# Sixteen unread products on TensorE in the routing stage of a two-block transformer kernel

## The chip, the cores and the metric

One core of a Trainium2 chip runs the whole kernel. The metric is the device time of one execution in microseconds, as the median of several runs. The granted clock of TensorE, which the profile gives as a share of full speed, has two levels: 0.50 (1.2 GHz) and 1.00 (2.4 GHz).

## The reference

Two blocks are computed one after the other on a sequence of 512 tokens of width 1024, in float32. The first is gated linear attention beside a convolution branch, the second is an mLSTM beside differential attention. The second block ends in an expert-choice feed-forward layer, and this is the part that matters here:

```
def expert_choice_ffn(h, w_router, w_gate, w_up, w_down):
    B, S, _ = h.shape
    cap = EC_CAPACITY * S // N_EXPERTS            # 2 * 512 / 16 = 64 tokens for each expert
    aff = jax.nn.softmax(jnp.einsum('bsd,de->bse', h, w_router).astype(jnp.float32), axis=-1)
    g, idx = lax.top_k(aff.transpose(0, 2, 1), cap)
    xe = h[bidx, idx]
    hid = (jax.nn.silu(jnp.einsum('becd,edf->becf', xe, w_gate))
           * jnp.einsum('becd,edf->becf', xe, w_up))
    ye = jnp.einsum('becf,efd->becd', hid, w_down) * g[..., None].astype(h.dtype)
    return jnp.zeros_like(h).at[bidx, idx].add(ye)
```

There are 16 experts, each with three weight matrices of 1024 x 2048 float32, so 24 MB of weights for each expert, 384 MB in all. The result is normalised and written out.

## The kernel before, in words

Every engine has one instruction stream of its own, written out by hand, and the streams wait for each other by counting semaphores (`t_dve`, `t_act`, `t_pe` in the routing, `x_...` and `e_...` in the experts). TensorE's stream has three stages.

**Dense blocks.** Up to about 1050 us TensorE multiplies the tiles of both blocks, mostly products of split operands (`d_hi`, `d_lo`) at line 2127.

**Routing**, from line 2405 to line 2434, about 1050 to 1068 us. `by_token` (line 2401) makes the router's logits in PSUM bank 3. `tokens_first` (line 2396) transposes the residual `xT` for one quarter of the tokens by eight transposes with the identity `ident`; three quarters go ahead of the ranking, the fourth, `tokens_first(3, 0)`, after it has been fed. ScalarE copies each quarter to `x2`, the tokens by row. VectorE computes the softmax `aff`; TensorE transposes it (line 2418, "affT"), and VectorE then ranks it: eight rounds of MAX8 (line 1931), with seven of MATCH_REPLACE8 (line 1933) between them, and three small steps that end in the limit `thr` for each expert (line 1936). TensorE waits for that at line 2422, transposes `thr` into bank 3 ("thrT", line 2423), VectorE marks the chosen tokens (lines 1939 and 1940), TensorE counts them by five products with a triangle and with ones (lines 2427 to 2432, "count"), and VectorE makes the positions `pos` and with them the selections `picks` (line 1954).

**Experts**, from line 2554. `gather(0)` (line 2442) multiplies `picks` by `x2`: eight products with 64 output partitions and 512 columns. ScalarE copies the result (`xg_first`), TensorE transposes it (line 2450), VectorE scales it to `xe` (line 1962), and then come the products with the weights, `gate_up` (line 2483) and `down` (line 2494), 64 and 32 of them for each expert, four for each 1 MB slot of weights. Each of them consists of two matmul records in the trace, and so does every product whose operands are plain float32; a transpose is one record.

The weights come on SyncE's queue alone, in the order of use, into a ring: `ring_a` and `ring_b` hold 22 slots of 1 MB, two more lie in `acc` and one in `once` (`ONCE = 3`, the fourth slot that is used). Filling starts long before the routing. The slots in `acc` wait for the last of the transposed tokens ("x3"), the one in `once` waits for "thrT". Every later transfer waits until TensorE has used the slot that it overwrites (`s_used`), the first of them until the first slot of expert 0 is used:

```
                    if g == ONCE:
                        sp.wait_ge(t_pe.sem, t_pe.count("thrT"))
                    elif order_of(g) >= RING + EXTRA:
                        sp.wait_ge(s_used, freed(g + n - 1))
```

All these waits of SyncE are in one order in one stream, the transfers too.

Of the kernel before, what the change touches and what calls it, by code (L numbers as in the profile page):

```python
# [14 lines left out]
S = 512  # L15
# [265 lines left out]
def kernel_program(nc, xT_in, pT_in, table, tri_in, gla_mask_in, rstm_in, negm_in, selr_in, m01_in, dist_in, tiles_in,  # L281
                   wgk_in, gkw_in, mgw_in, selg_in, diff_lam_2, w_router_2, experts_in, norm_f_g_2, x3_store, out):
    ctx = ExitStack()
    with ctx:
# [3 lines left out]
        def at(name, shape, kb, dt=F32):  # L288
            n = 4
            for d in shape[1:]:  # L290
                n *= d
            kb += 16 if kb >= 192 else 0
            assert base + kb * KB + n <= nc.sbuf_usable_end, (name, kb, n)
            return nc.alloc_sbuf_tensor_at(name, shape, dt, offset=base + int(kb * KB))
# [121 lines left out]
        x2 = at("x2", [P, TT, D], 64)  # L416
# [40 lines left out]
        ident = at("ident", [P, P], 192)  # L457
# [9 lines left out]
        ps = ctx.enter_context(nc.psum_tensor("ps", [P, 8, S], F32))  # L467
# [1555 lines left out]
        def _(pe):  # L2023
# [372 lines left out]
            def tokens_first(t, b):  # L2396
                for k in range(KD):
                    mm = pe.transpose(ps[:, b + k // 4, k % 4 * P:(k % 4 + 1) * P], xT[:, k, t * P:(t + 1) * P], ident[:, :])
                t_pe.done(mm, f"x{t}")

            def by_token(w, part, first):
                for t in range(TT):
                    tok = slice(t * P, (t + 1) * P)
                    mm = pe.matmul(ps[:, 3, t * 32:(t + 1) * 32], part[:, tok], w, start=first and t == 0, stop=True,
                                   skip_group_check=True)
                return mm

            pe.wait_ge(t_dve.sem, t_dve.count("part"))
            by_token(selm[:, :], lpart, True)
            read_done(pe, "out2", KD - 1)  # L2410
# [8 lines left out]
            t_pe.done(mm, "affT")  # L2419
            pe.wait_ge(t_act.sem, t_act.count("x0"))  # L2420
            tokens_first(3, 0)
            pe.wait_ge(t_dve.sem, t_dve.count("thr"))
            t_pe.done(pe.transpose(ps[:, 3, 0:NE], thr[:, 0:1].to_broadcast([NE, P]), ident[0:NE, 0:NE]), "thrT")
            pe.wait_ge(t_act.sem, t_act.count("ones"))
# [3 lines left out]
            for t in range(TT - 1):  # L2428
                pe.matmul(both[:, :, t + 1:, :], ones_r[:, :], chosen[:, :, t, :].unsqueeze(2).to_broadcast([P, 2, TT - 1 - t, NE]),
                          start=False, stop=False, skip_group_check=True)  # L2430
            pe.wait_ge(t_dve.sem, t_dve.count("gsum"))
            t_pe.done(pe.matmul(both[:, 1, :, :], ones[:, :], gsum[:, :].unsqueeze(1).to_broadcast([P, TT, NE]),
                                start=False, stop=True, skip_group_check=True), "count")
            pe.wait_ge(t_act.sem, t_act.count(f"x{TT - 1}"))

            def gather(e):
                if e >= 2:
                    pe.wait_ge(e_dve.sem, e_dve.count("o1", e - 2))
                for t in range(TT):
                    pe.wait_ge(x_dve.sem, x_dve.count(f"picks{t}", e))  # L2440
                    for d in range(2):
                        mm = pe.matmul(ps[d * CAP:(d + 1) * CAP, 5, :], picks[:, t, :], x2[:, t, d * S:(d + 1) * S],  # L2442
                                       start=t == 0, stop=t == TT - 1, skip_group_check=True)
                x_pe.done(mm, "gather")
# [281 lines left out]
```

## Time and profile before

| | |
|---|---|
| time, median of 3 runs | 1978.18 us (1977.48 to 1978.26) |
| the profiled execution: time | 1977.37 us |
| the profiled execution: span, first to last instruction | 1975.5 us |
| mean granted clock of TensorE | 0.99 |
| busy in the span | TensorE 96%, VectorE 37%, ScalarE 26%, GpSimd 3% |
| the chain that ended last | TensorE 73%, DMA 23%, ScalarE 2%, VectorE 1% |

The first lines say how long an execution takes; the time is 1.9 us more than the span in the profiled one. A busy share of TensorE says that its pipeline held a matmul, not that it ran at its peak. The chain is the sequence of work, followed back from the last instruction, in which each step released the next. In the rows below, an interval is given in microseconds from the span's start, PE is TensorE's matmuls, PEld its weight loads, DVE VectorE, ACT ScalarE, and SPq the transfers that SyncE issues. A name pair such as `ps<-x,picks` says which tensors an instruction writes and reads, and the shape behind it gives partitions and columns. What stands in square brackets at a row's end is how long the engine had been idle, and what released it.

### The profile page before, as it was taken

To read this page: it belongs to the slowest core of one execution; us is meant where nothing else is said; L and a number is where in the kernel's file an instruction comes from. 1 tells how busy PE (TensorE), PEld (TensorE's weight loads), DVE (VectorE), ACT (ScalarE), POOL (GpSimd) and SP (SyncE) were. 2 spreads that over 40 slices of the span, in tenths; PEclk is the share of its full clock that TensorE was granted. 3 is DMA by queue.
4 is the path that set the end of the run, shared out by engine and by line. 5 is a ranking of instruction groups with operands and counts; after the bars stand their busy time and mean duration, and the time that the engine had idled before them with its cause. 6 is when DMAs were issued, how large, how long until landed. Compare 5 with 4: busy or idle time off the path is not lost.

```text
span 1975.5 us, 20685 instructions
## 1 busy us (share of the span) xinstructions
PE 1888.2 (96%) x8735; PEld 1146.0 (58%) x8735; DVE 730.3 (37%) x1217; ACT 517.6 (26%) x837; POOL 61.2 (3%) x58
## 2 busy tenths in 40 slices
PE   8999999999999999999997999999888998989898
PEld 6788888888887888877874333333323333333332
DVE  7544444333356765777453111111111110111112
ACT  5444323222245353377622000000000000000002
POOL 1000000000014001100010000000000000000000
PEclk9999999999999999999998999999999999999999
DMA  5222322233322233121387999999999999999997
GB/s 189 86 86 64 118 96 96 96 98 98 109 94 100 82 109 127 55 71 46 138 329 306 421 433 431 432 432 433 434 432 432 432 432 434 432 432 432 431 429 295
DMA packets 49324, 504.93 MB, mean 256 GB/s; under 512 B 6416, under 2 KB 7440, under 8 KB 30544
## 3 DMA queue, kind: packets, MB, share of 16 engines
q1 hardware_dynamic: 48368, 502.49, 62.4%
q8 instruction: 69, 1.13, 0.2%
q10 hardware_dynamic: 864, 1.12, 0.2%
q14 instruction: 23, 0.19, 0.0%
HBM read 499.39 MB, written 4.19 MB: 255 GB/s over the span
## 4 chain that ended last, share of the span: by engine, by line
PE 73%; DMA 23%; ACT 2%; DVE 1%; issue 1%; ACTq 0%; SPq 0%; DVEq 0%
PE ps L2127 41%; DMA ring_a<-in_experts_in 23%; PE ps L2483 10%; PE ps L2494 6%; PE ps L2062 4%; PE ps L2442 3%; PE ps L2466 1%; PE ps L2304 1%; PE ps L2529 1%; PE ps L2280 1%; ACT hidT L1246 0%; PE ps L2505 0%; PE ps L2247 0%; PE ps L2230 0%; PE ps L2180 0%
## 5 line engine op out<-in xcount | busy, mean ns | idle before, releaser
L2483 PE MATMUL ps<-ring_a,xe 128*64 128x512 f32 x1504 | 343.0, 609 | 42.0 <-DMA ring_a<-in_experts_in 41.4
L2483 PEld LDWEIGHTS ps<-ring_a,xe 128*64 128x64 f32 x1504 | 107.0, 140 | 271.7 <-issue 211.9
L1291 DVE TENSOR_TENSOR d_lo<-d_raw,d_hi 128x1024 fp32r<-128x1024 f32 x166 | 206.1, 1250 | 120.4 <-ACT d_hi L851 119.5
L2127 PE MATMUL ps<-n_hi,d_hi 128*128 128x512 f32 x448 | 176.1, 393 | 1.5 <-DVE d_lo L1291 0.8
L2127 PE MATMUL ps<-n_lo,d_hi 128*128 128x512 f32 x448 | 174.4, 389 | 0.0
L2127 PE MATMUL ps<-n_hi,d_lo 128*128 128x512 f32 x448 | 174.3, 389 | 0.0
L851 ACT ACTIVATE d_hi<-d_raw 128x1024 fp32r<-128x1024 f32 x166 | 170.8, 1049 | 8.6 <-DMA d_raw<-in_tiles_in 6.4
L1521 DVE TENSOR_TENSOR hid<-hid,ps 128x512 f32<-128x512 f32 x32 | 20.7, 684 | 410.1 <-PE ps L2483 383.7
L1970 DVE TENSOR_TENSOR acc<-acc,ps 128x1024 f32<-128x1024 f32 x56 | 64.6, 1216 | 244.7 <-PE ps L2466 244.7
L2494 PE MATMUL ps<-ring_a,hidT 128*64 128x512 f32 x648 | 145.8, 596 | 9.3 <-DMA ring_a<-in_experts_in 6.2
L2483 PE MATMUL ps<-ring_b,xe 128*64 128x512 f32 x464 | 103.1, 594 | 3.0 <-DMA ring_b<-in_experts_in 2.9
L2494 PEld LDWEIGHTS ps<-ring_a,hidT 128*64 128x64 f32 x648 | 50.0, 137 | 90.3 <-issue 73.3
L2127 PEld LDWEIGHTS ps<-n_hi,d_hi 128*128 128x128 f32 x448 | 84.1, 188 | 19.7 <-DVE d_lo L1291 1.2
L2127 PEld LDWEIGHTS ps<-n_lo,d_hi 128*128 128x128 f32 x448 | 84.1, 188 | 17.5
L2127 PEld LDWEIGHTS ps<-n_hi,d_lo 128*128 128x128 f32 x448 | 84.1, 188 | 17.2
L2127 PE MATMUL ps<-h_hi,d_hi 128*128 128x512 f32 x224 | 89.4, 399 | 0.2 <-DVE d_lo L1291 0.2
L2127 PE MATMUL ps<-h_hi,d_lo 128*128 128x512 f32 x224 | 87.4, 390 | 0.0
L2127 PE MATMUL ps<-h_lo,d_hi 128*128 128x512 f32 x224 | 87.4, 390 | 0.0
L1237 ACT ACTIVATE xg<-ps 128x256 f32<-128x256 f32 x30 | 9.9, 382 | 292.9 <-PE ps L2442 292.9
L1243 ACT ACTIVATE hid<-ps 128x512 f32<-128x512 f32 x30 | 16.3, 594 | 258.7 <-PE ps L2483 258.7
L2483 PEld LDWEIGHTS ps<-ring_b,xe 128*64 128x64 f32 x464 | 33.0, 137 | 70.7 <-issue 65.8
L2494 PE MATMUL ps<-ring_b,hidT 128*64 128x512 f32 x304 | 68.2, 595 | 2.8 <-ACT hidT L1246 2.8
(505 smaller groups left out, 2719.9 us busy)
## 6 DMA issues: line engine op xcount, KB each, us to landing
ring_a<-in_experts_in SPq DMA_DIRECT2D x56, 4096.0 KB, 42.2
ring_b<-in_experts_in SPq DMA_DIRECT2D x28, 3072.0 KB, 42.5
d_raw<-in_tiles_in SPq DMA_DIRECT2D x166, 512.0 KB, 3.3
ring_a<-in_experts_in SPq DMA_DIRECT2D x31, 1024.0 KB, 12.9
ring_a<-in_experts_in SPq DMA_DIRECT2D x12, 2048.0 KB, 13.6
ring_b<-in_experts_in SPq DMA_DIRECT2D x5, 2048.0 KB, 13.5
ring_b<-in_experts_in SPq DMA_DIRECT2D x8, 1024.0 KB, 16.5
x_in<-in_xT_in SPq DMA_DIRECT2D x4, 512.0 KB, 7.2
```

What stands on the lines that cost most here:

```text
L851: act.activation(d_hi[:, n % SLOTS, :, :], d_raw[:, n % SLOTS, :, :], ACT.Copy).then_inc(t_hi, 1)
L1291: dve.tensor_tensor(d_lo[:, n % SLOTS, :, :], d_raw[:, n % SLOTS, :, :], d_hi[:, n % SLOTS, :, :].bitcast(F32), ALU.subtract).then_inc(t_l ...
L1521: return dve.tensor_tensor(out, a, b, ALU.mult)
L1970: e_dve.done(dve.tensor_tensor(row, old, ps[:, b:b + 2, :], ALU.add), f"o{t}")
L2062: mm = pe.matmul(bank, lt[:, k, t * P:(t + 1) * P], rhs, start=k == 0 and m == 0, stop=k == KD - 1 and m == 2)
L2127: mm = pe.matmul(bank, lt[:, n, gr.k0 + k, :], rt[:, k, :], start=k == 0 and m == 0, stop=k == gr.nk - 1 and m == 2)
L2280: mm = pe.matmul(ps[:, 5 + h % 2, q * P:(q + 1) * P], aaT[:, n % 2, c, :], d_tok[:, c, h * DDV:(h + 1) * DDV], start=c == 0, stop=c == TT - 1)
L2304: mm = pe.matmul(ps[:, 2 + i, :], dqT[half, h, q * P:(q + 1) * P], dkT[half, h, :], start=True, stop=True)
L2442: mm = pe.matmul(ps[d * CAP:(d + 1) * CAP, 5, :], picks[:, t, :], x2[:, t, d * S:(d + 1) * S], start=t == 0, stop=t == TT - 1, skip_group_ ...
L2466: return pe.matmul(ps[:, bank, :], place[half, t * P:(t + 1) * P], ye[half, :], start=start, stop=True, skip_group_check=True)
L2483: mm = pe.matmul(ps[half * CAP:(half + 1) * CAP, 2 * m + q, :], xe[:, k, :], slot(e, n)[:, (2 * q + half) * S:(2 * q + half + 1) * S], sta ...
L2494: mm = pe.matmul(ps[d * CAP:(d + 1) * CAP, 4, :], hidT[:, q, c, half * CAP:(half + 1) * CAP], slot(e, n)[:, j * D + d * S:j * D + (d + 1) ...
```

## The change

A helper `kept_busy(n)` issues n products of the identity (stationary) and the first 512 columns of the first quarter of `x2` (moving), all into PSUM bank 3, whose contents nobody reads. Fourteen stand between the last transposes of the tokens and the wait for `thr`, two between the counting products and `gather(0)`. Nothing else changes; no semaphore is signalled or awaited by them.

```
             def by_token(w, part, first):
...
+            def kept_busy(n):
+
+                for _ in range(n):
+                    pe.matmul(ps[:, 3, :], ident[:, :], x2[:, 0, 0:S], start=True, stop=True)
+
             pe.wait_ge(t_dve.sem, t_dve.count("part"))
...
             pe.wait_ge(t_act.sem, t_act.count("x0"))
             tokens_first(3, 0)
+            kept_busy(14)
             pe.wait_ge(t_dve.sem, t_dve.count("thr"))
             t_pe.done(pe.transpose(ps[:, 3, 0:NE], thr[:, 0:1].to_broadcast([NE, P]), ident[0:NE, 0:NE]), "thrT")
...
             t_pe.done(pe.matmul(both[:, 1, :, :], ones[:, :], gsum[:, :].unsqueeze(1).to_broadcast([P, TT, NE]),
                                 start=False, stop=True, skip_group_check=True), "count")
             pe.wait_ge(t_act.sem, t_act.count(f"x{TT - 1}"))
+            kept_busy(2)
 
             def gather(e):
```

TensorE's order in the routing before, from the last transposes of the tokens to the first products with weights (`thr` is the limit, `chosen` the marks, `gsum` their sums; x8 stands for eight in a row):

```order
L2398 MATMUL ps<-ident,xT 128x128 x8
L2423 MATMUL ps<-ident,thr 128x16
L2427 MATMUL ps<-chosen,tri_r 128x128
L2429 MATMUL ps<-chosen,ones_r 128x2x48
L2429 MATMUL ps<-chosen,ones_r 128x2x32
L2429 MATMUL ps<-chosen,ones_r 128x2x16
L2432 MATMUL ps<-gsum,ones 128x64
L2442 MATMUL ps<-x_161,picks 64x512 x8
L2450 MATMUL ps<-ident,xg_first 128x128 x4
L2483 MATMUL ps<-ring_a,xe 64x512 x12
```

The same place of the same engine after the change:

```order
L2398 MATMUL ps<-ident,xT 128x128 x8
L2411 MATMUL ps<-x_161,ident 128x512 x14
L2429 MATMUL ps<-ident,thr 128x16
L2433 MATMUL ps<-chosen,tri_r 128x128
L2435 MATMUL ps<-chosen,ones_r 128x2x48
L2435 MATMUL ps<-chosen,ones_r 128x2x32
L2435 MATMUL ps<-chosen,ones_r 128x2x16
L2438 MATMUL ps<-gsum,ones 128x64
L2411 MATMUL ps<-x_161,ident 128x512 x2
L2449 MATMUL ps<-x_161,picks 64x512 x8
L2457 MATMUL ps<-ident,xg_first 128x128 x4
L2490 MATMUL ps<-ring_a,xe 64x512 x12
```

The new rows are the two at line 2411. The order of everything else on TensorE, and that of ScalarE, VectorE and SyncE, is as before; line numbers behind the helper grow by five to seven.

## Rows read from the trace of the kernel before

**Rows 1.** The page: granted clock and GB/s in 40 slices of the span
```profile
PEclk9999999999999999999998999999999999999999
GB/s 189 86 86 64 118 96 96 96 98 98 109 94 100 82 109 127 55 71 46 138 329 306 421 433 431 432 432 433 434 432 432 432 432 434 432 432 432 431 429 295
```

**Rows 2.** The chain that ended last, 1076 to 1976 us: start, length, what
```profile
1076.15 27.69 PE ps L2483 x128
...
1319.45 37.34 DMA ring_a<-in_experts_in
...
1919.17 32.82 DMA ring_a<-in_experts_in
```

**Rows 3.** Timeline of TensorE, 1050 to 1085 us: start, length, then the instruction
```profile
1053.22 2.82 PE L2398 MATMUL ps<-ident,xT 128*128 128x128 f32 x24
...
1056.76 1.04 PE L2398 MATMUL ps<-ident,xT 128*128 128x128 f32 x8
1064.92 0.28 PE L2423 MATMUL ps<-ident,thr 16*128 16x16 f32 x1 [7.13 <-DVE thr L1936]
1065.82 0.45 PE L2427 MATMUL ps<-chosen,tri_r 128*128 128x128 f32 x1 [0.61 <-DVE chosen L1940]
1066.06 0.76 PE L2429 MATMUL ps<-chosen,ones_r 128*128 128x96 f32 x3
1066.66 0.67 PE L2432 MATMUL ps<-gsum,ones 128*128 128x64 f32 x2
1068.41 5.97 PE L2442 MATMUL ps<-x,picks 128*64 128x512 f32 x16 [1.08 <-DVE picks L1954]
...
1076.15 5.37 PE L2483 MATMUL ps<-ring_a,xe 128*64 128x512 f32 x24 [0.59 <-DVE xe L1962]
1081.35 1.89 PE L2483 MATMUL ps<-once,xe 128*64 128x512 f32 x8
```

**Rows 4.** Windows: busy time by engine, then granted clock, DMA share, GB/s
```profile
1053.00:1058.00 5.00, 4.32 (x38) 3.84 (x37) 2.87 (x13) 4.70 (x8) 0.17 (x2) 1.00 0.90 374
1069.00:1072.00 3.00, 3.00 (x10) 0.95 (x8) 0.27 (x1) 0.00 (x0) 0.00 (x0) 0.50 0.94 396
```

**Rows 5.** Short windows in which the granted clock falls and rises
```profile
1059.25:1059.50 0.25, 0.00 (x0) 0.00 (x0) 0.22 (x3) 0.25 (x3) 0.00 (x0) 0.91 0.15 66
1059.50:1059.75 0.25, 0.00 (x0) 0.00 (x0) 0.25 (x1) 0.21 (x2) 0.00 (x0) 0.50 0.57 197
...
1073.10:1073.20 0.10, 0.10 (x2) 0.00 (x0) 0.00 (x0) 0.00 (x0) 0.00 (x0) 0.95 0.00 0
```

**Rows 6.** Timeline of SyncE's transfer issues, 1040 to 1976 us
```profile
1065.24 0.33 SPq L714 DMA_DIRECT2D once<-in_experts_in  x1
1078.13 24.36 SPq L714 DMA_DIRECT2D ring_a<-in_experts_in  x10
```

**Rows 7.** Windows around the start of the experts and later
```profile
1076.00:1079.00 3.00, 2.85 (x14) 1.07 (x16) 0.43 (x2) 0.38 (x1) 0.00 (x0) 1.00 0.00 0
1079.00:1082.00 3.00, 3.00 (x16) 1.01 (x14) 0.00 (x0) 0.00 (x0) 0.00 (x0) 1.00 1.00 325
...
1097.00:1100.00 3.00, 3.00 (x16) 1.01 (x14) 0.00 (x0) 0.00 (x0) 0.00 (x0) 1.00 1.02 437
```

**Rows 8.** DMA issues, 1040 to 1130 us: size, us from issue to landing
```profile
once<-in_experts_in SPq DMA_DIRECT2D x1, 1024.0 KB, 7.6
```

**Rows 9.** Timeline: float32 products with 128 stationary columns, at full clock
```profile
1963.71 0.59 PE L2533 MATMUL ps<-acc,ident 128*128 128x512 f32 x1
...
1964.14 3.60 PE L2511 MATMUL ps<-ye,place 128*128 128x512 f32 x8
1964.57 0.19 PEld L2511 LDWEIGHTS ps<-ye,place 128*128 128x128 f32 x1 [0.24 <-issue]
```

**Rows 10.** Timeline of TensorE around 1921 us: a lone product with the identity
```profile
1920.39 1.12 PE L2533 MATMUL ps<-acc,ident 128*128 128x512 f32 x2
...
1921.44 1.94 PE L2483 MATMUL ps<-ring_a,xe 128*64 128x512 f32 x8
```

**Rows 11.** Timeline of TensorE: small products and the second gather, at full clock
```profile
1050.47 0.97 PE L2404 MATMUL ps<-selm,lpart 128*128 128x32 f32 x8
...
1103.67 3.60 PE L2442 MATMUL ps<-x,picks 128*64 128x512 f32 x16
```

More of the change, by code:

```diff
@@ L2406, in by_token, with kept_busy @@
                 return mm
+            def kept_busy(n):
+                for _ in range(n):
+                    pe.matmul(ps[:, 3, :], ident[:, :], x2[:, 0, 0:S], start=True, stop=True)
             pe.wait_ge(t_dve.sem, t_dve.count("part"))
@@ L2421, in _ @@
             tokens_first(3, 0)
+            kept_busy(14)
             pe.wait_ge(t_dve.sem, t_dve.count("thr"))
@@ L2434, in _ @@
             pe.wait_ge(t_act.sem, t_act.count(f"x{TT - 1}"))
+            kept_busy(2)
             def gather(e):
```

## The prediction

> **What bounds the kernel now.** I read the page's slices first, then the chain, then TensorE's timeline around the routing. In the slices [rows 1] the reader is to see one dip of the granted clock, in the 22nd slice (1037 to 1087 us), and behind that slice transfers at 421 to 434 GB/s almost to the end. That slice holds the routing and the start of the experts, so I asked short windows for the clock: 1.00 up to 1059.25 us, then 0.50 [rows 5] until 1073.1 us. What TensorE did before it fell: its last transposes ended at 1057.80 us, and then it stood still for 7.13 us, waiting for the limit `thr` [rows 3]. Before it rose, TensorE had worked on the gather from 1068.41 us, 4.7 us long. So the counting products and most of the first gather run at 1.2 GHz.
>
> The second question is what a shift of this place does to the end. The chain [rows 2] is TensorE's own work from the first product with weights on, and from 1319 us mostly transfers: the experts are bound by the weights. Before the first product with weights the ring is full: from 1076 to 1079 us the DMA moves nothing, and from 1079 us it is busy in every window [rows 7]. The transfer that restarts it was issued at 1078.13 us [rows 6], when the first slot of expert 0 had been used, 1.98 us after the first product with weights started [rows 3]. The pause is no reserve: all bytes behind it wait for that release. So the end moves by just what the start of `gate_up(0, 0)` moves by, and I only have to find that start.
>
> **The change, part by part.** Nothing is removed. The path from the transposes to the first product with weights is one line of work, so each edit is costed on it.
>
> *Fourteen products.* Each has 128 stationary columns, 512 moving ones and float32 operands, the form of the rows of the last products of the kernel [rows 9]: eight records take 3.60 us, and with a record's length of 0.59 us the start-to-start distance is (3.60 - 0.59) / 7 = 0.43 us. A weight load of 0.19 us stands every 0.43 us (0.19 + 0.24 idle) and hides beside the matmuls. A product is two records, 0.86 us, and fourteen are 28 x 0.43 = 12.04 us. They can start when the last transpose has started, 1057.80 - 0.27 us (a record of a transpose lasts 0.27 us), plus 0.13 us: 1057.66 us. The array is free for "thrT" at 1069.70 us. VectorE is not touched and has `thr` ready as before, when "thrT" started at 1064.92 us [rows 3]. The wait for `thr` covers 7.3 us of the products; the other 4.78 us lie on the path. **+4.78 us.** Queued behind them are "thrT" and the counting, and SyncE waits for "thrT" with the slot `once`: it was issued at 1065.24 us [rows 6] and landed 7.6 us later [rows 8], at 1072.8 us; issued 4.8 us later behind transfers that have drained by then, it lands at 1077.6 us even if it takes as long again, and is read at 1081.35 us before [rows 3], later now. That costs nothing.
>
> By the Trainium skill, "TensorE: Matmul & The Clock Gate", section "Back-to-back issue gap", a product of N columns takes N/2.4 + 2.5 ns at full clock, 216 ns here; by that fourteen would be over after 3.0 us, inside the wait, and the sum would be -3.0 us instead. The rows with float32 operands disagree with it (0.86 us), and I go by the rows.
>
> *The clock.* With products from 1057.66 us on without a pause I expect the clock to stay at 1.00 where it fell at 1059.5 us. The stretch before the products holds mainly transposes [rows 4], at 1.00 throughout.
>
> *The counting.* Six records lie between 1065.82 and 1067.33 us, 1.07 us from the first start to the last (1066.66 + 0.67 - 0.44 for the last record, less 0.22). At full clock small products with 128 stationary columns start about 0.10 to 0.12 us apart, eight in 0.97 us [rows 11], so five distances take 0.5 to 0.6 us, and the last record is shorter by about 0.17 us. Bounds: 0.3 us (the weight loads alone shrink) and 0.8 us (all of it halves). I take **-0.6 us**, nearest to the rows of the same width.
>
> *Two products.* Before, TensorE waited 1.08 us between the counting and the gather for VectorE's selections [rows 3]. The two products take 4 x 0.43 = 1.72 us and begin some 0.15 us before the counting's last record ends, so the gather can start 1.57 us after it: **+0.5 us**. From below, 0.4; from above, 0.7 with a change of form (a lone product between 64-column ones takes 1.05 instead of 0.86 us [rows 10]).
>
> *The first gather.* 5.97 us before [rows 3]; the second one, the same 16 records at full clock, 3.60 us [rows 11]: **-2.37 us**. The half-clock records show the factor: ten lie in the 3 us from 1069 [rows 4].
>
> *Behind it.* The copy, the transposes and the products with weights ran at full clock before, and do so now.
>
> **Sum.** 4.78 - 0.6 + 0.5 - 2.37 = **+2.3 us**. The profiled execution took 1977.37 us (span 1975.5 us), so it becomes 1979.7 us; the median of the runs is 0.8 us above it, and what is measured is a median: 1978.18 + 2.3 = **1980.5 us**, 0.12% more. With the bounds of the small terms it is +1.6 to +2.9 us. A measurement of this kernel tells about 0.2%, 4 us, from no change; the forecast is below that. The clock gives back 3.0 us, and the products past the end of the wait cost more than that.
>
> **Rivals.**
>
> *A: the products are cheap, and it is faster.* If a product cost what 64-column products cost, 0.2145 us a record (16 in 3.60 us, [rows 11]), fourteen would end at 1057.66 + 6.0 = 1063.7 us, before `thr`, and the two at 0.86 us would hide in the 1.08 us. Then -0.6 - 2.37 = -3.0 us: 1975.2 us. For it: every float32 product of the experts and of the gather goes at that pace. Against it: those rows are of 64 stationary columns, and the rows of the very form, with the identity as an operand too, go at half of it [rows 9, 10]. This rival also stands for the issue-gap rule quoted above. Chance 0.08.
>
> *B: the clock falls all the same, and it is slower.* The place is 1059.5 us: by then only 1.8 us of products have run, and before them there were transposes and short pauses. Falling there, the clock comes back after a stretch like the 4.7 us of the gather [rows 3, 5], counted from the first product or from the fall: at 1062.4 to 1064.2 us. Records at half clock take 0.86 us, so half of that stretch is lost: +1.5 to +2.3 us on the forecast, 1982.0 to 1982.8 us. Chance 0.09. If such products do not bring the clock up at all, the remaining 24 records cost 0.43 us more each (+10.2), the two products +1.7, and the gains of 3.0 us go: 1980.5 + 14.9 = 1995.4 us. Chance 0.03. It decides from the first window after 1059.5 us that shows less than 1.00. Against it: the clock fell only after TensorE had stood still for 1.7 us.
>
> The Trainium skill's "TensorE: Matmul & The Clock Gate", "Part 4: PE-mode transpose", says that transposes don't count as busy for the clock; that speaks for B. In this trace the clock stayed at 1.00 through them [rows 4].
>
> *C: each product costs as a lone one does,* 1.05 us [rows 10], because the form or the weight load breaks the pipeline: 14 x 1.05 = 14.7 us, +2.7 us on the forecast, 1983.2 us. Against it: the eight records in a row [rows 9]. Chance 0.08.
>
> *D: the shift is lost in the experts,* because the DMA's pace and not its restart sets the end: 1978.2 us. Against it: the DMA has no second pause after 1079 us in which it could catch up. Chance 0.07.
>
> **How the numbers follow.** The rivals have 0.08 + 0.12 + 0.08 + 0.07 = 0.35, and the forecast keeps 0.65, some 0.05 of it for small causes that nothing above names. The range from 1978.0 to 1983.2 us takes in the forecast, D, the short case of B and about half of C (which ends at its edge): 0.65 + 0.07 + 0.09 + 0.04 = 0.85, or 0.80 without the small causes. It leaves out A, the long case of B and the other half of C. Slower by over 0.2% means over 1982.1 us: most of the short B (0.06), its long case (0.03) and C as far as it is more than half right (0.06), with 0.02 of the small causes: 0.17. Faster by over 0.2%, under 1974.2 us, would need more than all that the clock can give back: 0.02. The rest, 0.81, is within 0.2%.
>
> **What would show it.** In the profile after: 28 records at the helper's line from 1057.7 us, 0.43 us apart; TensorE's wait for `thr` gone; "thrT" near 1069.7 us, with VectorE idle for about 4.8 us before its marks; the clock at 1.00 from 1050 to 1090 us; the first gather 3.6 us; the first product with weights 2.3 us later, near 1078.5 us; the DMA's restart as much later, near 1080.4 us; and the end shifted by the same. I am wrong if the wait for `thr` is still there (A), if any window there shows 0.50 (B), if the records are over 0.5 us apart (C), or if the restart shifts and the end does not (D).

## The result, and the profile after

The changed kernel took 1980.51 us in the median of 20 runs (1978.68 to 1983.36), the kernel before 1977.74 us in 20 runs beside it (1976.2 to 1980.75). The ratio is 1.0013, with a 95% interval from 1.0007 to 1.0018: some 2.6 us more (1.4 to 3.6), of which 2.3 were forecast. It is a small loss, within the 0.2% that the forecast called no change. The profiled execution took 1980.74 us, its span 1978.9 us; that is 3.4 us more than the span before, a little above the ratio, and the trace says why.

The slices of the changed kernel's page, as in [rows 1]:

```profile
PEclk9999999999999999999999999999999999999999
GB/s 189 86 85 64 118 96 97 99 97 102 107 89 107 75 117 119 64 65 52 144 327 280 424 428 431 432 433 432 433 433 433 431 431 432 433 434 432 431 429 296
```

The dip of the clock in the 22nd slice is gone. The 22nd slice of the transfers is lower (280 GB/s for 306), since the pause of the DMA that lies in it is longer. TensorE's timeline of the changed kernel, 1050 to 1090 us, with columns as in [rows 3]:

```profile
1053.13 4.48 PE L2398 MATMUL ps<-ident,xT 128*128 128x128 f32 x24
1057.45 0.38 PE L2423 MATMUL ps<-ident,affp 128*64 128x128 f32 x2
1057.67 1.04 PE L2398 MATMUL ps<-ident,xT 128*128 128x128 f32 x8
1058.54 12.18 PE L2411 MATMUL ps<-x,ident 128*128 128x512 f32 x28
1070.66 0.23 PE L2429 MATMUL ps<-ident,thr 16*128 16x16 f32 x1
1071.49 0.30 PE L2433 MATMUL ps<-chosen,tri_r 128*128 128x128 f32 x1 [0.60 <-DVE chosen L1940]
1071.62 0.45 PE L2435 MATMUL ps<-chosen,ones_r 128*128 128x96 f32 x3
1071.92 0.41 PE L2438 MATMUL ps<-gsum,ones 128*128 128x64 f32 x2
1072.17 1.94 PE L2411 MATMUL ps<-x,ident 128*128 128x512 f32 x4
1074.04 3.65 PE L2449 MATMUL ps<-x,picks 128*64 128x512 f32 x16
1078.18 0.71 PE L2457 MATMUL ps<-ident,xg_first 128*128 128x128 f32 x4 [0.48 <-ACT xg_first L1237]
1079.48 5.37 PE L2490 MATMUL ps<-ring_a,xe 128*64 128x512 f32 x24 [0.59 <-DVE xe L1962]
1084.68 1.89 PE L2490 MATMUL ps<-once,xe 128*64 128x512 f32 x8
```

The wait of 7.13 us for `thr` has no bracket any more: 28 records stand in its place, 12.18 us long, and it is VectorE that waits now. VectorE's timeline shows `thr` ready at 1065.79 us and the marks 5.2 us later; its first row is the copy of the logits, its last the step behind the counting:

```profile
1053.33 0.29 DVE L1913 COPY lraw<-ps 128x128 f32<-128x128 f32 x1 [2.06 <-PE ps L2404]
...
1065.58 0.21 DVE L1936 TENSOR_REDUCE thr<-least 16x1 f32<-16x65 f32 x1
1070.99 0.22 DVE L1939 TENSOR_TENSOR chosen<-aff,ps 128x64 fp32r<-128x64 f32 x1 [5.21 <-PE ps L2429]
...
1072.38 0.29 DVE L1521 TENSOR_TENSOR counted<-chosen,ps 128x128 f32<-128x128 f32 x1 [0.87 <-PE ps L2438]
```

The first gather takes 3.65 us for 5.97. Windows of the changed kernel, with columns as in [rows 4], show the clock and the DMA:

```profile
1052.50:1053.00 0.50, 0.50 (x7) 0.50 (x7) 0.00 (x0) 0.50 (x1) 0.00 (x0) 1.00 0.72 295
1053.00:1053.50 0.50, 0.50 (x6) 0.50 (x6) 0.17 (x1) 0.43 (x2) 0.14 (x2) 0.89 1.16 492
1056.50:1057.00 0.50, 0.50 (x5) 0.50 (x4) 0.01 (x1) 0.41 (x1) 0.00 (x0) 0.69 0.96 389
1057.00:1075.00 18.00, 17.39 (x61) 8.54 (x61) 9.67 (x35) 3.06 (x5) 0.00 (x0) 1.00 0.76 300
...
1079.00:1082.00 3.00, 2.52 (x12) 0.92 (x14) 0.76 (x2) 0.70 (x1) 0.00 (x0) 1.00 0.02 5
1082.00:1085.00 3.00, 3.00 (x16) 1.01 (x14) 0.00 (x0) 0.00 (x0) 0.00 (x0) 1.00 0.70 268
```

From 1057 us on the clock is full. But it had been at half for 3.4 us just before, from 1053.4 to 1056.8 us, while TensorE made the first 24 transposes, which took 4.48 us for 2.82 [rows 3]. That is ahead of every added product, and it made the ranking and all that follows 1.0 us later. The DMA restarts after 1082 us, where it did so at 1079 us [rows 7]. SyncE's issues:

```profile
1070.91 0.33 SPq L714 DMA_DIRECT2D once<-in_experts_in  x1
1081.46 24.36 SPq L714 DMA_DIRECT2D ring_a<-in_experts_in  x10
```

The issue that restarts it is 3.33 us later than in [rows 6], as the first product with weights is (1079.48 for 1076.15), and the span is 3.4 us longer. The slot `once`, issued 5.7 us later than before, landed 4.7 us after its issue, at 1075.6 us, and was first used at 1084.68 us: that delay cost nothing.

### The profile page after: what moved, and what is told of

It reads as the page before. It is cut to its first block, busy times and chain, and to the rows that moved or that the text cites. A ratio compares the mean times of both kernels' runs of the same rounds, so it can differ in the third digit from the quotient of the medians.

```text
span 1978.9 us, 20748 instructions
## 1 busy us (share of the span) xinstructions
PE 1903.2 (96%) x8767; PEld 1153.5 (58%) x8767; DVE 729.8 (37%) x1217; ACT 517.8 (26%) x837; POOL 61.1 (3%) x58
## 4 chain that ended last, share of the span: by engine, by line
PE 73%; DMA 23%; ACT 1%; DVE 1%; issue 1%; ACTq 0%; SPq 0%; DVEq 0%
PE ps L2127 41%; DMA ring_a<-in_experts_in 23%; PE ps L2490 10%; PE ps L2501 6%; PE ps L2062 4%; PE ps L2449 2%; PE ps L2473 2%; PE ps L2411 1%; PE ps L2304 1%; PE ps L2280 1%; PE ps L2536 1%; PE ps L2512 0%; PE ps L2247 0%; PE ps L2230 0%; PE ps L2177 0%
```

## The experiments

Each leaves the kernel's result as it is. The numbers behind the edits are of the function `kept_busy`. All but four were timed in turns with the kernel before, in 11 executions (five with twenty products), and have a ratio to it with its 95% interval. The four are single executions for a second or third profile. A single execution scatters by some 2 us either way, so the profiles are read by distances inside one execution, collected in the table behind the experiments. For a change of 1 to 3 us the times alone say little more than its sign.

### Eight products instead of fourteen

```
-            kept_busy(14)
+            kept_busy(8)
```

> Eight products before the wait for the limit instead of fourteen, two before the gather. Theory Q (the products block TensorE for 0.86 us each, and only what lies past the end of the wait for thr costs time): eight take 6.9 us and end inside the wait of about 7.1 us, so thrT starts when thr is ready, as before; the clock stays at 1.00; counting -0.6, gather -2.3, the two products +0.6: the first product with weights 2.3 us earlier than before and 5.1 to 5.6 us earlier than with fourteen; time 0.12% under before. Theory W (the change costs time because the slot once and the transfers start later or TensorE's reads disturb the weights, not by blocking): the time stays near that with fourteen, since the products are still there.

1976.26 us against 1977.97, ratio 0.999 (0.9981 to 0.9999). TensorE's timeline:

```profile
1057.34 7.03 PE L2411 MATMUL ps<-x,ident 128*128 128x512 f32 x16
1064.64 0.22 PE L2429 MATMUL ps<-ident,thr 16*128 16x16 f32 x1 [0.27 <-DVE thr L1936]
...
1066.16 1.94 PE L2411 MATMUL ps<-x,ident 128*128 128x512 f32 x4
1068.03 3.65 PE L2449 MATMUL ps<-x,picks 128*64 128x512 f32 x16
```

A wait of 0.27 us for `thr` is left: eight products of this form are just what the wait holds. The products are still there and the time is below that of before, so theory W falls; blocking is what the fourteen cost. The first product with weights came 20.33 us after the copy of the logits, 2.2 us sooner than in the middle one of three profiles of the kernel before (22.55) and 5.8 sooner than in the changed kernel's, 1.0 of which is the early fall. The ranking itself was not disturbed: from the start of "affT" to `thr` it took 8.33 to 8.37 us in all fourteen profiles.

### Twenty instead of fourteen

```
-            kept_busy(14)
+            kept_busy(20)
```

> Twenty products before the wait instead of fourteen. Theory Q: six more take 12 x 0.43 = 5.15 us, all of it past the end of the wait, and the end moves by as much: 5.1 us over the changed kernel, 7.7 us (0.4%) over before. Theory D (the experts' transfers set the end and absorb a shift of the routing): thrT moves by 5.1 us and the end by clearly less.

1984.52 us against 1977.97, ratio 1.0034 (1.0021 to 1.0047), by the ratio 6.7 us over before (4.2 to 9.3), of 7.7 forecast. The products and what restarts the transfers, in the timelines of TensorE and SyncE:

```profile
1057.25 17.33 PE L2411 MATMUL ps<-x,ident 128*128 128x512 f32 x40
1074.51 0.23 PE L2429 MATMUL ps<-ident,thr 16*128 16x16 f32 x1
```

```profile
1085.31 0.33 SPq L714 DMA_DIRECT2D ring_a<-in_experts_in  x1
```

12 records more take 5.15 us more (17.33 for 12.18), and from the first product with weights to the end it is 899.37 us as with fourteen (899.42). Theory D falls: the experts absorb nothing that can be told here.

### Without the two before the gather

```
-            kept_busy(2)
```

> The fourteen products stay, the two before the gather are taken out. Theory Q: the gather starts 1.04 us after the start of VectorE's counted, as before, instead of 1.66 us; all else as with both; the clock stays at 1.00; 0.6 us less than the changed kernel. Rival (the two are needed to hold the clock over the wait for the selections): the clock falls in or before the gather, and the gather takes up to 6 us instead of 3.65.

1981.39 us against 1977.97, ratio 1.0016 (1.0007 to 1.0025): no gain over both, as the rival had it. The clock fell in the pause before the gather, as the gather's row and windows of the profile show:

```profile
1072.03 5.29 PE L2448 MATMUL ps<-x,picks 128*64 128x512 f32 x16 [1.08 <-DVE picks L1954]
```

```profile
1069.50:1071.50 2.00, 0.85 (x6) 0.74 (x6) 1.00 (x5) 0.00 (x0) 0.00 (x0) 1.00 0.41 86
1071.50:1072.00 0.50, 0.00 (x0) 0.00 (x1) 0.46 (x3) 0.00 (x0) 0.00 (x0) 0.96 0.93 393
1072.00:1075.00 3.00, 2.97 (x8) 1.11 (x10) 0.88 (x4) 0.00 (x0) 0.00 (x0) 0.50 0.54 227
```

The gather starts 0.6 us sooner after the counting and takes 5.29 us for 3.65: 1.0 us lost in sum (9.83 for 8.82 us from "thrT" to the first product with weights). A second profile was to tell whether that is so each time:

> Fourteen and none, looked at again. In its first profile the clock fell just before the gather, with eight and none it did not, though the pauses are the same. Theory P: here it may stay, and then the first product with weights comes 8.2 us after thrT instead of 9.83. Rival (something in fourteen makes it fall always): 9.8 us again.

It fell again, at 1072.8 us, this time 0.7 us inside the gather, and the distance was 9.88 us:

```profile
1072.50:1073.00 0.50, 0.50 (x4) 0.17 (x2) 0.41 (x2) 0.00 (x0) 0.00 (x0) 0.79 1.16 492
```

That is the number of the rival, but two profiles of two don't show that it falls always.

### Only the two before the gather

```
-            kept_busy(14)
```

> Only the two products between the counting and the gather. The clock has fallen by then as before. Theory Q: the two take 4 x 0.86 = 3.4 us at half clock against a wait of 1.08 us, so the gather starts 2.2 us later than before; the clock comes back inside the gather at about the time at which it came back before, so the gather is shorter by 1.2 to 2 us: net +0.2 to +1.0 us. Rival (two products are enough to bring the clock back before the gather): the gather takes 3.7 us, and the net is near zero.

1978.29 us against 1977.97, ratio 1.0001 (0.9992 to 1.001). TensorE's timeline, and windows on the clock:

```profile
1066.74 3.33 PE L2411 MATMUL ps<-x,ident 128*128 128x512 f32 x4
1070.00 3.65 PE L2448 MATMUL ps<-x,picks 128*64 128x512 f32 x16
```

```profile
1066.50:1069.50 3.00, 3.00 (x6) 1.36 (x6) 1.82 (x7) 0.00 (x0) 0.00 (x0) 0.50 1.01 426
1069.50:1070.00 0.50, 0.50 (x2) 0.00 (x0) 0.00 (x0) 0.00 (x0) 0.00 (x0) 0.96 1.12 475
```

The two took about what was said (3.33 us for 3.4), but they brought the clock back ahead of the gather and not inside it, so the rival was right: the gather takes 3.65 us, and gain and cost cancel.

### Eight and none, eight and one

```
-            kept_busy(14)
+            kept_busy(8)
...
-            kept_busy(2)
```

> Eight products before the wait for the limit, none before the gather. Theory Q, as it stands after the first runs (only products past the end of a wait cost time, 0.86 us each; the clock is a second, separate account): the gather starts 1.04 us after counted instead of 1.66 us. If the clock stays at 1.00, the first product with weights comes 8.2 us after thrT (8.82 us with both fillers) and the time is 0.6 us under that with eight and two. If it falls in the pause between the counting and the gather, as it did with fourteen and none, 9.8 us after thrT, and the time is 1.0 us over that with eight and two. I take the second for the likelier, since the pauses are the same as there.

1975.02 us against 1978.05, ratio 0.9987 (0.9978 to 0.9996). My likelier case was wrong: the clock stayed at 1.00 through the gather, from 1057 to 1072 us,

```profile
1057.00:1072.00 15.00, 12.57 (x46) 5.51 (x44) 9.16 (x33) 3.31 (x7) 0.00 (x0) 1.00 0.86 351
```

and the first product with weights came 8.19 us after "thrT". The pauses behind the products are those of fourteen and none, plus 0.27 us ahead of "thrT". This is one profile, and why the clock held here and fell there is open. The next has `kept_busy(8)` and `kept_busy(1)`:

> Eight products before the wait and one before the gather. Theory Q: one product takes 0.86 us and ends before VectorE's selections are there (1.08 us), so the gather starts 1.04 us after counted, as without it; with the clock held, the first product with weights comes 8.2 us after thrT, 0.6 us less than with eight and two, and the time is 3.0 to 3.3 us (0.16%) under before. Rival: one product does not hold the clock, it falls in the gather, and the distance is 9 us or more.

1975.99 us against 1978.05, ratio 0.9989 (0.998 to 0.9998). From "thrT" on it was as forecast (8.11 us), but the clock fell early here too, 0.7 us into the first token transposes, from 1054.6 to 1058.0 us, which costs 1.0 us in the profile:

```profile
1054.50:1055.00 0.50, 0.50 (x5) 0.50 (x4) 0.43 (x3) 0.43 (x2) 0.00 (x0) 0.55 0.89 377
```

### The products at the cheap price

```
-                for _ in range(n):
-                    pe.matmul(ps[:, 3, :], ident[:, :], x2[:, 0, 0:S], start=True, stop=True)
+                for i in range(n):
+                    half = i % 2
+                    pe.matmul(ps[half * CAP:(half + 1) * CAP, 3, :], ident[:, 0:CAP], x2[:, 0, 0:S], start=True, stop=True,
+                              skip_group_check=True)
```

> The same fourteen and two products, each with 64 stationary columns instead of 128, turn by turn into the two halves of bank 3. This puts the cheap price of rival A to the test: 0.2145 us a record as in the gather. Theory Q: fourteen take 6.0 us and end before thr, two take 0.86 us and end before the selections; thrT as before, with a wait of about 1.1 us ahead of it; the first product with weights 8.2 us after thrT if the clock holds; time 3.0 us under before. Rival W (products beside the ranking disturb it or the transfers): the ranking takes longer than its 8.4 us from affT to thr, or the time is not under before.

1975.54 us against 1978.05, ratio 0.9992 (0.9983 to 1.0). In TensorE's timeline the same number of records takes half the time:

```profile
1057.41 6.23 PE L2412 MATMUL ps<-x,ident 128*64 128x512 f32 x28
1064.61 0.22 PE L2431 MATMUL ps<-ident,thr 16*128 16x16 f32 x1 [0.98 <-DVE thr L1936]
```

The clock stayed at 1.00. This is rival A made real, and its sum (-3.0 us) is what the profile shows: 19.61 us from the logits to the first product with weights, for 22.38, 22.55 and 22.73 in the three profiles of the kernel before. The times show less of it, 1.6 us by the ratio, with an interval from nothing to 3.4 us.

### Transposes instead of products

```
-                for _ in range(n):
-                    pe.matmul(ps[:, 3, :], ident[:, :], x2[:, 0, 0:S], start=True, stop=True)
+                for i in range(n):
+                    pe.transpose(ps[:, 3, i % 4 * P:(i % 4 + 1) * P], x2[:, 0, i % 4 * P:(i % 4 + 1) * P], ident[:, :])
...
-            kept_busy(14)
+            kept_busy(56)
...
-            kept_busy(2)
+            kept_busy(8)
```

> The fourteen products are replaced by 56 transposes of the same data (0.11 to 0.12 us each, 6.3 us in all) and the two by 8 (0.9 us). The blocking is the same as with eight products and one. Theory T (transposes count for the clock as products do; those at the end of the routing ran at 1.00 before the change, and in the changed kernel the clock came back while only transposes ran): the clock stays at 1.00, the first product with weights comes 8.2 us after thrT, time 3 us under before. Rival S (transposes do not count as busy, as the Trainium skill's TensorE page says in its part on PE-mode transpose): the clock falls during them or soon after and the first product with weights comes 11 us after thrT as before; time as before or 0.5 us over.

1975.87 us against 1978.05, ratio 0.9991 (0.9982 to 0.9999). The profile shows each theory half right. Windows:

```profile
1053.50:1056.00 2.50, 2.50 (x13) 2.50 (x13) 1.25 (x7) 2.41 (x4) 0.00 (x0) 0.50 1.01 416
1056.50:1058.00 1.50, 1.50 (x15) 1.50 (x15) 0.34 (x1) 1.48 (x2) 0.00 (x0) 1.00 0.45 169
1058.50:1064.50 6.00, 6.00 (x57) 5.87 (x54) 5.55 (x20) 1.42 (x3) 0.00 (x0) 1.00 0.80 310
1066.50:1067.00 0.50, 0.50 (x4) 0.50 (x4) 0.00 (x0) 0.00 (x0) 0.00 (x0) 0.70 1.04 442
```

The clock came back to 1.00 after 3.5 us in which TensorE had done nothing but transposes (1052.9 to 1056.5 us), and held through 56 more. Then it fell 2 us behind the last of them, in the counting, and was back inside the gather: 9.54 us from "thrT" to the first product with weights, more than the 8.2 of theory T and far from the 11 of rival S. So transposes do count for the clock: in the kernels whose TensorE had stood still in the wait for `thr`, it came back only 10 us or more after it had fallen. Whether they count as much as products stays open, since it fell behind them.

### The kernels before and changed, profiled again

> The kernel before, looked at again. Open: in the changed kernel's profile, in that with eight and one and in that with transposes, the clock fell for 3.4 us just before or at the start of the token transposes, ahead of all added products, and affT came 1.0 us later; in the other profiles it did not. Theory P (where a fall comes after the same work is a matter of chance, and the change has no part in it): it can show in this kernel as well, and if it does, the first product with weights comes 1.0 us later after the logits. Rival: it belongs to kernels with added products alone, and never shows here.

> The same as the last, once more: a second chance to see the early fall in a kernel without added products.

> The changed kernel, looked at again. Theory P: with the chance of some 3 in 10 the early fall shows again; if it does not, affT comes 3.1 us after VectorE has read the logits instead of 4.1, thrT starts 16.2 us after that instead of 17.3, and the end is 1 us earlier relative to the logits. The rest, from thrT to the first product with weights, is 8.82 us in either case.

The changed kernel had no early fall this time, and its first product with weights came 25.15 us after the logits for 26.15; "thrT" stood 16.32 us behind them, as forecast (16.2). Its window from 1050 us on:

```profile
1050.00:1085.00 35.00, 32.84 (x150) 16.80 (x151) 13.02 (x47) 9.95 (x15) 0.17 (x2) 1.00 0.66 253
```

The two new profiles of the kernel before showed no early fall either. The fall in the wait for `thr` moved: it was at 1059.5 us in the first profile and at 1061.7 and 1062.1 us in these.

### The distances in one table

In us, within each profiled execution: from VectorE's copy of the logits to "thrT", from there to the first product with weights, their sum, and from that product to the span's end.

| kernel | to thrT | on to weights | sum | to the end |
|---|---|---|---|---|
| before | 11.50 | 11.23 | 22.73 | 899.35 |
| before, second profile | 11.51 | 10.87 | 22.38 | 899.09 |
| before, third profile | 11.51 | 11.04 | 22.55 | 900.65 |
| changed: 14 and 2 | 17.33 | 8.82 | 26.15 | 899.42 |
| changed, second profile | 16.32 | 8.83 | 25.15 | 899.25 |
| 8 and 2 | 11.51 | 8.82 | 20.33 | 898.94 |
| 20 and 2 | 21.48 | 8.82 | 30.30 | 899.37 |
| 14 and 0 | 16.34 | 9.83 | 26.17 | 899.40 |
| 14 and 0, second profile | 16.33 | 9.88 | 26.21 | 900.33 |
| 0 and 2 | 11.51 | 10.89 | 22.40 | 899.06 |
| 8 and 0 | 11.51 | 8.19 | 19.70 | 899.89 |
| 8 and 1 | 12.50 | 8.11 | 20.61 | 899.33 |
| halves, 14 and 2 | 11.50 | 8.11 | 19.61 | 899.78 |
| transposes, 56 and 8 | 12.50 | 9.54 | 22.04 | 898.93 |

The first column is the products' blocking, in steps of 0.43 us a record, with the early fall (1.0 us) in three rows. The second is the clock's doing, and where two products of the full price stand before the gather, 0.6 us is theirs (8.82 for 8.19). The last lies between 898.9 and 900.7 us while the sum varies by 10.7 us: the end follows the first product with weights.

## Why the prediction was right, point by point

*Fourteen products, +4.78 us.* Without the early fall: 16.32 - 11.51 = 4.81 us. The record distance was 0.43 us, as in [rows 9].

*The clock stays at 1.00.* So it did, from the products on, in both profiles. But the text also promised 1.00 from 1050 us on, and called any window there with 0.50 a sign of rival B. That sign did show, from 1053.4 to 1056.8 us in the first profile, from a cause that is not B's; it was too broad.

*The counting, -0.6 us.* From the first counting product to VectorE's next step 1.55 us before and 0.89 us after (1071.49 to 1072.38): -0.66, and -0.07 more between "thrT" and the counting. The row of before:

```profile
1067.37 0.29 DVE L1521 TENSOR_TENSOR counted<-chosen,ps 128x128 f32<-128x128 f32 x1 [1.53 <-PE ps L2432]
```

*The two products, +0.5 us.* From that step to the gather 1.04 us before, 1.66 after: +0.62.

*The gather, -2.37 us.* From its start to the transposes behind it 6.44 us before and 4.14 after (1074.04 to 1078.18): -2.30. This term has a scatter that I didn't count: in the other profiles of the kernel before the clock came back sooner in the gather, and it took 5.62 and 5.79 us. The forecast went by the longest of the three.

*One for one to the end.* Shown by the last column.

The sum was +2.3 us; the changed kernel's profile without an early fall and the middle one of the three of before differ by 25.15 - 22.55 = 2.6 us, and the runs by 2.6 us. That these two agree so well is partly luck: against the other two profiles of before it is 2.4 and 2.8 us, and the interval of the runs is 1.4 to 3.6 us. What carries the forecast is that each term came out.

The one thing in the profile that the text did not foresee is the fall in the token transposes. It put "thrT", the first product with weights and the restart of the DMA 1.0 us behind the places named (1070.66, 1079.48 and 1081.46 us for 1069.7, 1078.5 and 1080.4). I had put rival B's fall at 1059.5 us, behind these transposes.

Three readings in the prediction were wrong without harm. The bounds of the small terms add up to +2.0 and +2.8 us, not +1.6 and +2.9. The "less 0.22" in the counting's start-to-start distance belongs to nothing, as 1066.89 - 1065.82 is 1.07 without it. And the ten records of [rows 4] don't show the factor of two beside the sixteen of [rows 7], since a window also counts records that only end in it; the gather's term rested on [rows 11].

The rivals: A and C fall by the record distances, D by the twenty products and the last column, and B by the windows, which show no fall behind the first product. The Trainium skill's sentence on transposes ("TensorE: Matmul & The Clock Gate", "Part 4: PE-mode transpose") does not agree with these traces: transposes alone brought the clock from 0.50 to 1.00 in three profiles. The Trainium skill's 216 ns for a product of 512 columns (same page, "Back-to-back issue gap") is a quarter of the 0.86 us that a float32 product with 128 stationary columns took here. It is near what the split operands of the dense blocks show: those products, of the type `fp32r` and as wide, start 0.23 to 0.24 us apart, as in the kernel before:

```profile
1049.08 0.40 PE L2127 MATMUL ps<-m_hi,d_hi 128*128 128x512 f32 x1
1049.31 0.40 PE L2127 MATMUL ps<-m_hi,d_lo 128*128 128x512 f32 x1
```

What the change was worth: the clock gave back 3.0 us, and the products past the end of the wait took 4.8, the two at the gather 0.6. Eight and none has the gain without the cost: 0.9987 (0.9978 to 0.9996), 2.6 us under before. The changed kernel, timed at another time, had 1.0013 (1.0007 to 1.0018), so eight and none is the faster of the two as well. Eight and two, eight and one, the halves and the transposes can't be told from it by their times.

Open: whether the early fall comes more often in kernels with added products. It showed in three of ten profiles of them and in none of four without more than the two. What stands ahead of it is the same in all, so I take it for chance, but fourteen profiles don't settle it. Open too: why the clock fell at the gather with fourteen and none, twice, and not with eight and none, once.

## What to carry to other kernels

Work that keeps TensorE's clock up is free only as long as the wait that it fills, so its price must be read from a row of the same form, operand type and stationary width included, before it is counted out (0.24, 0.43 and 0.86 us for 512 columns here); past the end of the wait it costs its full length. Where the next stage is bound by transfers that wait for TensorE's first use of a slot, a pause of the DMA is no reserve: here every microsecond passed through to the end. Such fillers are worth little here (3 us of 1978), and a few that end just inside the wait did as well as any other choice.

## What the runs showed of the hardware

TensorE's clock did not fall at a fixed distance behind its last work: with the same idle time it fell 1.7, 4.4 and 4.7 us behind the last transposes in three executions of the kernel before. It fell in the pause before the gather and, in another execution, 0.7 us into the gather with fourteen products ahead, and did not with eight ahead and the same pause. And it fell without any idle time, at 1053.4, 1054.6 and 1053.1 us in three profiles, where TensorE had for 2.7 us done only products with 32 moving columns and then, for 0.1 to 0.7 us, transposes; in the other eleven it did not fall there, after the same work. In each of the six short falls of these profiles it was at half for 3.4 us, with products running or with transposes; where TensorE had stood still in the wait for `thr` it was at half for 13.6 us once and 10.2 us three times. A float32 product of 512 columns took 0.86 us with 128 stationary columns and 0.43 us with 64 in alternate halves.
